# A hybrid decoder step on one core: the key cache arrives with each page's features ahead of its tokens, and the page transposes go

## What is computed

```python
past_k = cache_k[layer][page_table].reshape(db, -1, N_KV_HEADS, HEAD_DIM)
past_v = cache_v[layer][page_table].reshape(db, -1, N_KV_HEADS, HEAD_DIM)
z = einsum('bqhgd,bshd->bhgqs', q * SB_SCALE, past_k) + bias
w = stick_breaking_weights(z, mask)      # exp(log_sigmoid(z) + sum of log_sigmoid(-z) over later keys)
out = einsum('bhgqs,bshd->bqhgd', w, past_v) + ...
```

## Time and profile before

| | us |
|---|---|
| median of 3 runs | 2072.54 |
| the profiled execution | 2068.06 |
| its span, first to last instruction | 2066.3 |
| PE busy / DVE busy / ACT busy | 1893.2 / 1195.7 / 941.9 |

### The profile page before, as it was taken

How to read it: one execution, slowest core, us unless ns; L and a number is a source line. 1 busy time by engine, 2 the same in 40 slices (tenths; PEclk the granted TensorE clock), 3 DMA queues, 4 the chain that set the end, 5 groups by cost and what they waited for, 6 DMA issues and landing times. The chain is left out here.

```text
span 2066.3 us, 41234 instructions
## 1 busy us (share of the span) xinstructions
PE 1893.2 (92%) x14730; PEld 1752.5 (85%) x14730; DVE 1195.7 (58%) x2001; ACT 941.9 (46%) x1547; POOL 191.7 (9%) x97
## 2 busy tenths in 40 slices
PE   6998999989898989999897988999999999999984
PEld 5897878778786878788786888999999999999983
DVE  6101667758585667768585443765666566655653
ACT  5121777766767577776766332222222122212213
POOL 0121000000000000000000001221122112211210
PEclk8999999989899999999998997999999999999998
DMA  3334213141322313141312301210111111111102
GB/s 132 114 82 117 75 46 97 40 105 37 89 60 79 84 39 102 40 108 41 90 51 83 134 1 50 62 51 30 51 51 51 38 43 51 51 41 41 51 10 98
DMA packets 196332, 135.25 MB, mean 65 GB/s; under 512 B 57999, under 2 KB 187600, under 8 KB 196144
## 3 DMA queue, kind: packets, MB, share of 16 engines
q1 hardware_dynamic: 196170, 133.15, 22.8%
HBM read 120.03 MB, written 13.32 MB: 65 GB/s over the span
## 5 line engine op out<-in xcount | busy, mean ns | idle before, releaser
L87 PE MATMUL d_p_up<-n_hi,d_w_hi 128*128 128x344 f32 (+1 forms) x1056 | 341.1, 323 | 17.3 <-POOL d_w_lo L1872 15.0
L87 PE MATMUL d_p_up<-n_lo,d_w_hi 128*128 128x344 f32 (+1 forms) x1056 | 340.7, 323 | 0.0
L87 PE MATMUL d_p_up<-n_hi,d_w_lo 128*128 128x344 f32 (+1 forms) x1056 | 339.0, 321 | 0.0
L2020 DVE TENSOR_TENSOR mix<-mix,d_p_down 128x344 f32<-128x344 f32 (+1 forms) x264 | 135.8, 515 | 262.1 <-PE d_p_down L2066 262.1
L87 PE MATMUL b_p_proj<-n_hi,b_w_hi 128*128 128x350 f32 x768 | 268.8, 350 | 16.2 <-DVE b_w_lo L1114 9.4
L87 PE MATMUL b_p_proj<-n_lo,b_w_hi 128*128 128x350 f32 x768 | 255.3, 332 | 0.0
L87 PE MATMUL b_p_proj<-n_hi,b_w_lo 128*128 128x350 f32 x768 | 254.9, 332 | 0.0
L1872 POOL TENSOR_TENSOR d_w_lo<-w_raw,d_w_hi 128x1024 fp32r<-128x1024 f32 x45 | 109.0, 2423 | 1488.5 <-ACT d_w_hi L1901 1488.5
L1916 ACT ACTIVATE d_up<-d_p_up 128x346 f32<-128x346 f32 x132 | 60.1, 456 | 392.2 <-PE d_p_up L87 391.2
L87 PEld LDWEIGHTS d_p_up<-n_hi,d_w_hi 128*128 128x128 f32 x1056 | 200.4, 190 | 18.4 <-POOL d_w_lo L1872 15.4
L87 PEld LDWEIGHTS d_p_up<-n_hi,d_w_lo 128*128 128x128 f32 x1056 | 201.2, 191 | 0.0
(11 more groups left out here) (263 smaller groups left out, 3877.4 us busy)
## 6 DMA issues: line engine op xcount, KB each, us to landing
w_raw<-in_w_in SPq DMA_DIRECT2D x45, 512.0 KB, 5.1
w_raw<-in_w_up SPq DMA_DIRECT2D x45, 512.0 KB, 3.9
b_page<-in_cache_k SPq DMA_DIRECT2D x128, 128.0 KB, 2.2
b_page<-in_cache_v SPq DMA_DIRECT2D x128, 128.0 KB, 2.1
w_raw<-in_w_down SPq DMA_DIRECT2D x22, 512.0 KB, 3.3
b_q_in<-q_scr SPq DMA_DIRECT2D x272, 32.0 KB, 2.2
mix<-in_x_prompt SPq DMA_DIRECT2D x8, 512.0 KB, 7.2
w_raw<-in_w_out SPq DMA_DIRECT2D x8, 512.0 KB, 3.3
```

Source lines behind the costliest of these rows:

```text
L87: last = pe.matmul(out, w[:, k, :], x[:, k, col:col + width], start=(k == 0 and w is w_hi and x is x_hi), stop=(k == KT - 1 and w is w_lo))
L2020: dve.tensor_tensor(to, to, p_down[:, n % 4, 0:width], ALU.add).then_inc(down_out, 1)
```

## The change

The host hands `cache_k` over transposed within each page: a page's 128 rows are features (two key heads of 64), its 256 columns are two such pairs by 128 tokens. A page's DMA still brings 128 rows of 1 KB. PE then takes the page itself as the stationary operand of the score products, at slot j+1. Gone are the transposes (L1403), ACT's copy (L1063), `k_t`, and PE's waits for `kt_out` and, at slots 2 to 9 other than 3, for `av_out`. The room of `k_t` becomes a third page buffer. Loads are moved: each waits for the pair that lay in its buffer (`page_before`), three pairs are loaded at the turn's start, pairs 11 to 14 at slots 14 and 15, and only pair 15 behind the first loads of the next turn. `p_zd` moves from `p_misc` into `p_kt`. DVE reads it at slot 9 instead of 10, and PE waits for that read before the scores of block 16, at the end of its slot 9, instead of at slot 11.

```diff
-PAGES_AT = {**{s + 1: (s + 2,) for s in range(8)}, 14: (10, 11), 15: (12, 13)}
+PAGES_AT = {**{s: (s + 2,) for s in range(1, 9)}, 14: (11, 12), 15: (13, 14)}
+PAGE_AT = tuple(j % 3 for j in range(15)) + (1,)
+
+def page_before(j):
+    return j - next(n for n in range(1, PAGES) if PAGE_AT[(j - n) % PAGES] == PAGE_AT[j])
+
+def page_users(j):
+    return [u for u in range(PAGES) if PAGE_AT[u] == PAGE_AT[j]]
...
-        page = sb("b_page", [P, 2, 2, KVH * HD])
-        k_t = sb("b_k_t", [P, 4, P])
+        page = sb("b_page", [P, 3, 2, KVH * HD])
...
-        p_zd = p_misc[:, 256:512].rearrange("p (h n) -> p h n", n=PAGES)
+        p_zd = p_kt[:, 0:256].rearrange("p (h n) -> p h n", n=PAGES)
...
-                    sp.wait_ge(page_used, nth(i, 16, j))
+                    sp.wait_ge(page_used, nth(i, 16, page_before(j), 4))
...
                     load_pages(i, 0)
                     load_pages(i, 1)
+                    load_pages(i, 2)
...
-                def last_pages(i):
-                    for j in (14, 15):
-                        load_pages(i, j)
+                def last_page(i):
+                    load_pages(i, 15)
...
                         score_out(i, s, first)
-                        if 2 <= s <= 9:
-                            act.wait_ge(page_used, nth(i, 16, s - 2, 2))
-                            act.activation(k_t[:, :, :].rearrange("p a c -> p (a c)"), p_kt[:, :],
-                                           ACT.Copy).then_inc(kt_out, 1)
...
-                        if s == 10:
+                        if s == 9:
                             decode_scores_out(i)
...
                     pe.wait_ge(z_copied, nth(i, SLOTS, s))
+                    if b == 16:
+                        pe.wait_ge(zd_read, nth(i, 1, 0))
...
-                    if n == 0 and s == 7:
-                        pe.wait_ge(zd_read, nth(i, 1, 0))
...
-                    if 2 <= s <= 9 and (not first or s > LAG):
-                        pe.wait_ge(av_out, nth(i, SLOTS, s - LAG - 1, 1))
                     if s == 3 and not first:
+                        pe.wait_ge(av_out, nth(i, SLOTS, -1, 1))
                         pick_heads(i)
...
-                    if 2 <= s <= 9:
-                        j = s - 2
-                        pe.wait_ge(kt_out, nth(i, 8, j))
-                        for n in range(2):
-                            for pair in range(2):
-                                last = pe.matmul(p_zd[:, 8 * pair:8 * (pair + 1), 2 * j + n], k_t[:, 2 * n + pair, :],
-                                                 g.q_block[:, pair, bass.ds(i, 1), :].rearrange("p a h -> p (a h)"),
-                                                 start=True, stop=True)
-                        last.then_inc(zd_done, 1)
                     if 1 <= s <= 8:
                         j = s - 1
-                        pe.wait_ge(page_arr[j % 2], 32 * nth(i, 8, j // 2))
+                        users = page_users(j)
+                        pe.wait_ge(page_arr[PAGE_AT[j]], 32 * nth(i, len(users), users.index(j)))
                         if s == 1:
                             pe.wait_ge(vd_copied, nth(i, 1, 0))
                         for n in range(2):
                             for pair in range(2):
-                                r = 2 * n + pair
-                                last = pe.transpose(p_kt[:, P * r:P * (r + 1)],
-                                                    page[:, j % 2, n, P * pair:P * (pair + 1)], g.ident[:, :])
+                                last = pe.matmul(p_zd[:, 8 * pair:8 * (pair + 1), 2 * j + n],
+                                                 page[:, PAGE_AT[j], n, P * pair:P * (pair + 1)],
+                                                 g.q_block[:, pair, bass.ds(i, 1), :].rearrange("p a h -> p (a h)"),
+                                                 start=True, stop=True)
                         last.then_inc(page_used, 1)
...
+        if name == "cache_k":
+            x = x.reshape(N_PHYS, PAGE, 2, 2, HD).transpose(0, 3, 4, 2, 1).reshape(N_PHYS, P, 2 * PAGE)
```

More of the change, by code:

```diff
@@ L839, in phase_mix @@
         gw_arr = sem("b_gw_arr")
-        page_arr = [sem(f"b_page_arr{s}") for s in range(2)]
+        page_arr = [sem(f"b_page_arr{s}") for s in range(3)]
         page_used = sem("b_page_used")
@@ L857, in phase_mix @@
         av_out = sem("b_av_out")
-        kt_out = sem("b_kt_out")
-        zd_done = sem("b_zd_done")
         zd_read = sem("b_zd_read")
@@ L886, in load_pages @@
                 def load_pages(i, j):
-                    cache = g.cache_k if j < 8 else g.cache_v
+                    cache = g.cache_k if j < 8 else g.cache_v[0].rearrange("n t h d -> n t (h d)")
                     numbers = [sp.value_load(g.table[0:1, bass.ds(i * PAGES + (2 * (j % 8) + n), 1)],
                                              min_val=0, max_val=N_PHYS - 1) for n in range(2)]
-                    sp.wait_ge(page_used, nth(i, 16, j))
+                    sp.wait_ge(page_used, nth(i, 16, page_before(j), 4))
                     for n in range(2):
-                        src = cache[0].rearrange("n t h d -> n t (h d)")[bass.ds(numbers[n], 1), :, :]
-                        sp.dma_start(page[:, j % 2, n, :], src.rearrange("a t c -> (a t) c"))\
-                          .then_inc(page_arr[j % 2], 16)
+                        sp.dma_start(page[:, PAGE_AT[j], n, :],
+                                     cache[bass.ds(numbers[n], 1), :, :].rearrange("a p c -> (a p) c"))\
+                          .then_inc(page_arr[PAGE_AT[j]], 16)
                 def load_q(i, s):
@@ L961, in group_loads @@
                     first_loads(group * 2 + 1, group, False)
-                    last_pages(group * 2)
+                    last_page(group * 2)
                     turn_loads(group * 2 + 1, group, False, None if last else group + 1)
@@ L965, in group_loads @@
                         first_loads(group * 2 + 2, group + 1, True)
-                    last_pages(group * 2 + 1)
+                    last_page(group * 2 + 1)
                 group_loads(0, False, True)
@@ L1206, in decode_scores_out @@
                 def decode_scores_out(i):
-                    dve.wait_ge(zd_done, nth(i, 8, 7))
+                    dve.wait_ge(page_used, nth(i, 16, 7, 4))
                     dve.tensor_tensor(zd, p_zd, g.bias_all[:, :].unsqueeze(2).to_broadcast([P, HEADS, PAGES]),
@@ L1214, in decode_sum_out @@
                 def decode_sum_out(i):
-                    dve.wait_ge(page_used, nth(i, 16, -1, 2))
+                    dve.wait_ge(page_used, nth(i, 16, -1, 4))
                     dve.tensor_copy(vacc, p_vd).then_inc(vd_copied, 1)
@@ L1293, in _ @@
                 for s, n in ((proj_done, CHUNK_NS), (qk_done, SLOTS), (wt_turned, GROUPS), (av_group, GROUPS),
-                             (page_used, 2)):
+                             (page_used, 4)):
                     pe.sem_inc(s, n)
@@ L1370, in decode_values @@
                             pe.wait_ge(wd_ready, nth(i, 1, 0))
-                        pe.wait_ge(page_arr[j % 2], 32 * nth(i, 8, 4 + j // 2))
+                        users = page_users(8 + j)
+                        pe.wait_ge(page_arr[PAGE_AT[8 + j]], 32 * nth(i, len(users), users.index(8 + j)))
                         for n in range(2):
@@ L1374, in decode_values @@
                             last = pe.matmul(p_vd[32 * (m % 4):32 * (m % 4 + 1), :], zd_wide[:, :, m],
-                                             page[:, j % 2, n, :], start=(m < 4), stop=(m >= PAGES - 4))
+                                             page[:, PAGE_AT[8 + j], n, :], start=(m < 4), stop=(m >= PAGES - 4))
                         last.then_inc(page_used, 1)
                 def decode(i, s, first):
-                    if 2 <= s <= 9 and (not first or s > LAG):
-                        pe.wait_ge(av_out, nth(i, SLOTS, s - LAG - 1, 1))
                     if s == 3 and not first:
+                        pe.wait_ge(av_out, nth(i, SLOTS, -1, 1))
                         pick_heads(i)
@@ L2309 @@
     for name in _INS:
-        x = np.ascontiguousarray(inputs[name])
+        x = inputs[name]
+        if name == "cache_k":
+            x = x.reshape(N_PHYS, PAGE, 2, 2, HD).transpose(0, 3, 4, 2, 1).reshape(N_PHYS, P, 2 * PAGE)
+        x = np.ascontiguousarray(x)
         arrays[f"in_{name}"] = x
```

## The result

The kernel after takes 2039.7 us (median of 4 runs, 2038.9 to 2042.2), beside 2072.3 for the kernel before (4 runs, 2068.7 to 2080.4): the ratio is 0.984, its 95% interval 0.982 to 0.987. The forecast was 2054, its range 2036 to 2068. So the sign was right and the time lay in the range, but the gain was 33 us where 18 were forecast. Between the two profiled executions the span went from 2066.3 to 2038.3, 28.0 us, and it is these that the traces can explain.

A forecast was written before the change was run, and what follows sets the result against it. PE was taken as the bound (busy 1893 of 2066 us), its saving paid only where DVE, ACT or SP isn't last. Terms of 25.3 us less 7 for the clock gave 18 off: 2050 profiled, 2054 as median, range 2036 to 2068.

The forecast's parts named there:

- PE's work per slot: A slot with transposes and score products pays 1.37 us and will pay 0.88: 0.49 saved, in slots 2 to 8.
- Slots 8 to 10: Turns 1 to 7: DVE is late, PE gains nothing and loses 0.2 us; slot 10's stall grows from 0.92 to 2.5.
- wait for `zd_read`: PE's new wait before the scores of block 16: between 0 and 0.2 us, inside the 2.5 already counted.
- The slower rival: DVE reads `p_zd` only after its slot-9 scan and argument, delaying block 16's scores: 2083 us, chance 0.05.
- the one that the saving is paid out in full: All of PE's saved work, its stalls and two half-clock stretches count: 51 us off, 2021 us, chance 0.05.
- Fresh turns: Turns 2, 4, 6: SP is last, values land as far behind slot 15; only slots 4 to 7 gain, 1.8 us each.
- SP is not last: In fresh turns slots 1 to 3 pay too, also stalls and two half-clock stretches: 30 us off, 2042 us, chance 0.12.
- The term of the clock: Five of seven slot-10 stalls followed by half clock, 1.2 us each on average: -6; with other turns' stretches together -7.
- the long class of stretches: Half-clock stretches of 6.8 us, loss 3.4, beside short ones of 3.4 us, loss 1.7, behind slot 10's stall.
- Turn 0: No RG-LRU tail on DVE and no stall at slot 10 there, so the turn gains 4.0 us.
- Waits for value pages: PE's 7.8 us of stalls for value pages should go, below 1 us in all; 2.9 us of it counted as gain.
- Turn 7's end: The tail behind turn 7 has 2.4 us of value-page stalls, of which 2.2 should be gained.

The follow-up runs named there:

- e3: Kernel after with the odd half of the new values loaded at SP's slot 1, ahead of two page pairs, with its own semaphore: 2020.7 us, ratio 0.975.
- e10: The kernel after again, unedited, on another chip: 2039.4 us, ratio 0.987.
- e9: Kernel after with value page pair 12 loaded at SP's slot 15 instead of 14, PE's code unchanged: 2040.7 us, ratio 0.987.
- e5: Kernel after with decode scores in the old bank, read at DVE's slot 10, and odd new values loaded at SP's slot 1: 2012.7 us, ratio 0.973.
- e11: Kernel after with 128 semaphore increments on PE ahead of turn 0: 2059.8 us, one execution.
- e12: Kernel after with 256 semaphore increments on PE ahead of turn 0: 2080.2 us, one execution.
- e2: Kernel after with the decode scores back in the old bank and DVE's read of them back in slot 10: 2028.4 us, ratio 0.981.

## Why the prediction was right, and where it was wrong

**What held.** PE's work per slot: 1.95 us in four slots, by the forecast 4 x 0.49. Slots 8 to 10: the forecast had a stall of 2.5, 0.2 lost, and no wait for `zd_read` above 0.2; measured were 2.4, 0.18 and none. The slower rival (the read of `p_zd` behind the scan) therefore fell, and so did the one that the saving is paid out in full. That the time lay in the range is in part luck: 28.8 - 18.2 = 10.6 us of the gain in the mix phase were not in the forecast, and most of them come from the terms below.

**Fresh turns: the mechanism held, one term was off.** The distance from the scores for slot 16 to slot 4 was to stay and shrank by 2.0, 0.4 and 0.8 us. The stalls at `b_v_odd` were 5.25, 7.67 and 2.96, forecast 6 to 7, above 3 and 1.5. SP sets this distance in both kernels, and its own walk became shorter, which the forecast had at nothing. Its last wait for PE ends 0.14 us after PE starts the scores for slot 16, in all three of these turns and both kernels. From there to the second issue for `b_v_odd` SP took 42.4, 45.5 and 38.7 us before and takes 40.3, 45.2 and 38.0 now, for the same seven page pairs: 2.1, 0.4 and 0.7 less. The profile after shows SP issuing for turn 6:

```profile
887.51 0.57 SPq L801 DMA_DIRECT2D b_v_odd<-v_scr  x1
888.12 0.43 SPq L802 DMA_DIRECT2D b_v_odd<-v_scr  x1
890.24 1.13 SPq L902 DMA_DIRECT2D b_page<-in_cache_k  x2
```

After 888.12 the next pair is again 2.1 us away, as before. By the rule of the Trainium skill (DMA: Bandwidth & Descriptors, Issuing engines are not separate DMA queues) this time should usually be small beside the transfer; here the queue's order set three stalls of 15.9 us in all, and e3, which passes two pairs, took them away. The rival "SP is not last" named 2042 us, near the time measured, but for a reason that did not occur.

**The term of the clock was mis-sized: -6 forecast, -1.4 measured.** Five of seven stalls in slot 10 were followed by half clock, just as assumed. Stretches of the kernel after, in this order: behind slot 10's stall in turns 3 and 4, across the `b_v_odd` stall of turn 4, behind slot 10's stall in turn 6 (PE, PEld, DVE, ACT, POOL busy, granted clock, DMA share, GB/s):

```profile
589.60:593.00 3.40, 3.40 (x46) 3.21 (x47) 3.37 (x7) 1.76 (x4) 0.00 (x0) 1.00 0.06 12
711.80:715.00 3.20, 3.20 (x13) 3.20 (x12) 3.17 (x8) 3.02 (x5) 0.00 (x0) 0.50 0.00 0
667.40:677.40 10.00, 5.71 (x40) 5.60 (x41) 3.81 (x9) 2.05 (x3) 0.00 (x0) 0.50 0.38 88
930.20:933.40 3.20, 3.20 (x24) 2.96 (x23) 3.17 (x8) 2.28 (x4) 0.00 (x0) 0.50 0.02 5
```

In this trace each fall in slots 10 to 16 lasted some 3.4 us, and PE does 1.7 us less in it. The second trace (e10) has falls in the same five turns, one of them twice as long, in turn 5:

```profile
815.70:822.30 6.60, 6.26 (x47) 6.03 (x48) 6.39 (x12) 4.49 (x7) 0.00 (x0) 0.50 0.03 7
```

There the term is -2.1 us. In the first trace slots 10 to 16 grew by only 0.2 to 0.3 us in these five turns, because PE used to wait 0.98 for `r_gr` and now comes later: in all five of these turns that wait is gone, in turns 3 and 7 it is still 0.98. I had averaged in the long class of stretches; the short one would have given 5 x (1.7 - 0.98) = 3.6, still too much, and why less was lost is open. In fresh turns the clock did what was forecast: slots 4 to 10 gained 0.1 instead of 5.3.

**A term was missing: the edge of the loop; it paid next to nothing.** The prediction read the waits of PE and passed over the row "issue", 20.5 us. They are now 9.4 + 3.7: the first wait shrank with the earlier landing of pair 13, which the forecast had priced by PE's page stalls alone, and the second came with the place of the code. But what fell away at the edge came back at `b_z` (+6.9), and in the fresh turns SP is last. Edge and `b_z` waits together, into turns 3, 5 and 7, are 16.1 us before and 17.4 after. Into turns 1, 3 and 7 the stretches gained 1.2, 5.9 and 2.4 us, and the terms of the forecast give 1.1, 6.0 and 2.1. The surplus of 3.4 is turn 5's: 4.0 gained, 0.9 forecast. There the clock differs. Two half-clock stretches of the kernel before in that turn, then the same part of the turn in the kernel after:

```profile
769.00:772.40 3.40, 3.40 (x25) 3.28 (x22) 2.39 (x5) 2.78 (x3) 0.00 (x0) 0.50 0.28 84
779.30:782.60 3.30, 3.30 (x18) 3.20 (x14) 2.83 (x5) 3.30 (x6) 0.00 (x0) 0.50 1.13 304
```

```profile
751.00:785.00 34.00, 29.18 (x314) 25.73 (x314) 21.36 (x36) 29.25 (x40) 0.00 (x0) 1.00 0.40 103
```

In e10, with one such stretch there, turn 5 gained 2.8; in e9, with 6.8 us of half clock as before, 2.2. So of the surplus some 1.8 is the clock, and 1.3 stays open.

**Smaller misses.** Turn 0 gained 1.5 less than forecast. Its slots 10 to 16 became 0.9 longer, in e10 too: ACT's `r_gr` is late there as well (a new wait of 0.63). By e10, whose slots 0 to 3 are shorter, turn 0 gained 3.9, as forecast. Waits for value pages were to be under 1 us and are 4.8 in four stalls of 0.4 to 1.9. Turn 7's end gained 1.6 more: the granted clock from its first product behind the turn's end to the next phase rose from 0.63 to 0.81. The 4.6 us between the gain by medians (32.6) and by the two spans (28.0) comes from the kernel before, whose profiled execution (2068.06) lay 4.2 under its median; its medians on three other sets of 7 to 16 runs, 2067.1 to 2069.5, lie nearer to it.

## What to carry to other kernels

Before costing a removed step, list for each place who is last next, and look at every wait row, also those put down to "issue": at a loop's edge the branch has a record of its own on PE's sequencer (3.4 to 4.0 us here), and how much of it PE waits for hangs on how early the sequencer gets there. A load that lands just ahead of the branch takes that lead away, and an edit that only shortens the code ahead of the loop can add a second wait. To compare two versions fairly, pad the code with idle instructions once or twice and see how far the time moves by that alone (here the kernel after by 2 to 12 us beside the padding's own cost). A saving that turns into a stall (slot 10, slot 4 of the fresh turns) is not lost: moving one read or one load past the place, as e5 did, paid another 27 us.

## What the hardware showed unexpectedly

The instruction queue's packets (queue, kind: packets, MB, share of 16 engines) in the whole trace of the kernel after, and at the edge between turns 3 and 4 of the kernel before, 644.5 to 645.5 us, and of the kernel after, 626.5 to 627.5 and 629.5 to 630.5:

```profile
q8 instruction: 94, 1.54, 0.3%
```

```profile
q8 instruction: 1, 0.02, 7.8%
```

```profile
q8 instruction: 1, 0.02, 5.5%
...
q8 instruction: 1, 0.02, 7.9%
```

1.54 MB in 94 packets are 16.4 KB for one; if a packet is the period of 256 instructions of e11 and e12, an instruction has 64 bytes, an estimate. That the waits are fetches of code is argued from these packets and that period. In the kernel before PE's last value-page product ends at 643.96 and it goes on at 647.49; in the kernel after it ends at 628.34 and goes on at 629.97, with the first packet already under way while it still worked.

The clock was not a function of the stall alone: the same stall of 2.40 in slot 10 was followed by full clock in turns 3 and 7 and by half clock in the other five, at the same work of PE. The stall of 1.75 was followed by half clock in four turns of seven in e2 and in none in e5.

PE's first product of the phase waited 15.9 us with 64 increments ahead of it, 25.9 with 128 and 45.5 with 256: 0.154 us for one (29.6 / 192). With 32 it waited 11.0, where the kernel after waits 9.4 for DVE, and the first scores began only 0.06 later.
